# Level products of the gated attention over two chunks at once, selected straight into the block diagonal matrix

## What is computed

```python
def gla_mixer(q, k, v, low, r, w_gate_up, b_gate, norm):
    # per head: S_t = exp(g_t) * S_(t-1) + k_t v_t^T ;  o_t = q_t S_t
    # g_t is a log decay for every one of the 64 key channels
    # inside a chunk: A[t, s] = sum_c q[t,c] k[s,c] exp(b[t,c] - b[s,c]) for s <= t,
    #   with b the running sum of the log decays in the chunk
    ...
y_a = gla_mixer(g_q, g_k, g_v, g_low, g_r, ...) @ w_branch_gla
y_b = swa_mixer(s_q, s_k, s_v, swa_sinks) @ w_branch_swa
y_c = pool_mixer(p_u, pool_w, pool_scale) @ w_branch_pool
gate = sigmoid(gates)
merged = gate[0] * y_a + gate[1] * y_b + gate[2] * y_c
x = x + rmsnorm(merged @ w_out)
```

## Time and profile before

| | |
|---|---|
| median of 3 runs | 1386.88 us |
| span of the profiled execution | 1384.7 us |
| profiled execution with what lies around its span | not listed apart; the median of the runs is 2.2 us above the span |
| TensorE busy | 1376.5 us (99%) |
| VectorE busy | 846.0 us (61%) |
| ScalarE busy | 603.8 us (44%) |
| GpSimd busy | 180.3 us (13%) |
| levels of the first pair of heads | 184 to 211 us from the span's start |
| levels of the second pair | 256 to 281 us |

### The profile page before, as it was taken

The page is one execution under the profiler, slowest core; times in us unless marked ns, Lnnn a source line. Parts: engine busy times, 40 slices in busy tenths (PEclk is TensorE's granted clock), DMA queues, the critical chain, the costliest instruction groups (busy, mean ns, idle before and its releaser), DMA issues.

```text
span 1384.7 us, 17291 instructions
## 1 busy us (share of the span) xinstructions
PE 1376.5 (99%) x6788; PEld 1121.1 (81%) x6788; DVE 846.0 (61%) x1231; ACT 603.8 (44%) x923; POOL 180.3 (13%) x149
## 2 busy tenths in 40 slices
PE   9999999999999999999999999999999999999998
PEld 8777777778888888888888887888888888788887
DVE  6565565855343798623776456646455575877775
ACT  5354432433235564423444345434544445344551
POOL 0300010212212300000000122000001220243330
PEclk9999999999999999999999999999999999999999
DMA  6322222223252423333233324322124233222132
GB/s 211 120 77 76 77 62 77 77 77 90 93 171 88 137 92 113 98 109 90 93 93 106 107 77 153 109 90 76 62 62 167 87 109 113 92 61 60 48 137 76
DMA packets 37553, 135.38 MB, mean 98 GB/s; under 512 B 4432, under 2 KB 5344, under 8 KB 36960
## 3 DMA queue, kind: packets, MB, share of 16 engines
q1 hardware_dynamic: 37328, 134.28, 30.7%
q10 hardware_dynamic: 144, 0.00, 0.0%
HBM read 127.97 MB, written 6.29 MB: 97 GB/s over the span
## 4 chain that ended last, share of the span: by engine, by line
PE 91%; DVE 6%; issue 1%; ACT 1%; DMA 0%; POOL 0%; DVEq 0%; ACTq 0%; SPq 0%; POOLq 0%
PE ps L204 89%; PE ps L208 3%; DVE TT L163 2%; DVE WL L151 2%; DVE HL L163 1%; DVE X L151 1%; DVE KT L163 0%; DVE sm L169 0%; DMA raw<-in_wall 0%; ACT HH L201 0%; ACT VT L201 0%; ACT WH L188 0%; DVE QT L163 0%; DVE KT L151 0%; ACT sm L201 0%
## 5 line engine op out<-in xcount | busy, mean ns | idle before, releaser
L204 PE MATMUL ps<-HH,WH 128*128 128x512 f32 (+1 forms) x1096 | 438.0, 401 | 0.7 <-DVE HL L163 0.6
L204 PE MATMUL ps<-HH,WL 128*128 128x512 f32 (+1 forms) x1096 | 424.1, 389 | 0.0
L204 PE MATMUL ps<-HL,WH 128*128 128x512 f32 (+1 forms) x1096 | 423.3, 388 | 0.0
L151 DVE TENSOR_TENSOR WL<-raw,WH 128x1024 fp32r<-128x1024 f32 (+1 forms) x223 | 286.2, 1288 | 79.7 <-ACT WH L188 78.5
L188 ACT CAST WH<-raw 128x1024 fp32r<-128x1024 f32 (+1 forms) x222 | 230.9, 1042 | 131.3 <-PE ps L204 109.2
L204 PEld LDWEIGHTS ps<-HH,WH 128*128 128x128 f32 x1096 | 205.9, 188 | 49.6 <-issue 7.9
L204 PEld LDWEIGHTS ps<-HH,WL 128*128 128x128 f32 x1096 | 205.8, 188 | 43.6
L204 PEld LDWEIGHTS ps<-HL,WH 128*128 128x128 f32 x1096 | 206.2, 188 | 41.3 <-issue 1.7
L204 PE MATMUL ps<-PH,WH 128*128 128x512 f32 x424 | 167.5, 395 | 0.0
L204 PE MATMUL ps<-PH,WL 128*128 128x512 f32 x424 | 165.2, 390 | 0.0
L204 PE MATMUL ps<-PL,WH 128*128 128x512 f32 x424 | 165.1, 389 | 0.0
(11 more groups left out here) (221 smaller groups left out, 1454.7 us busy)
## 6 DMA issues: line engine op xcount, KB each, us to landing
raw<-in_wall SPq DMA_DIRECT2D x221, 512.0 KB, 3.6
kept<-PW SPq DMA_DIRECT2D x2, 2048.0 KB, 8.9
PWR<-kept SPq DMA_DIRECT2D x2, 2048.0 KB, 7.6
X<-in_xT SPq DMA_DIRECT2D x8, 256.0 KB, 4.2
X<-in_xT SPq DMA_DIRECT2D x4, 512.0 KB, 5.0
out_T<-X SPq DMA_DIRECT2D x7, 256.0 KB, 2.0
pe<-in_pT SPq DMA_DIRECT2D x2, 512.0 KB, 5.1
DM<-in_dm SPq DMA_DIRECT2D x1, 640.0 KB, 3.9
```

What stands on the lines that cost most here:

```text
L151: return self.put(None if self.e is None else self.e.tensor_tensor(out, x, y, op))
L204: return self.put(None if self.e is None else self.e.matmul(out, l, r, start=start, stop=stop, skip_group_check=True))
```

## The change

What it does:

- PE takes one product for two neighbouring chunks of a head: 64 key channels, 128 keys, 128 queries. There are 4 products a head and level where there were 8, each with four times the results; half of these, keys of one chunk with queries of the other, are thrown away by the mask. The two heads of the pair take turns, product by product, in place of one after the other. A head's result fills its bank, 128 partitions by 512 columns.
- DVE picks with masks of 128 x 128 straight into gAbd, 512 columns an instruction. Level 0 multiplies by the identity of 128 columns that the kernel has anyway and so writes the zeros too. gA, idm, ACT's four copies and POOL's clearing of gAbd are gone. DVE's first picking of the second pair waits until PE has read gAbd of the first (`go`, 1), where it waited for ACT's copy.
- The masks are 384 KB in place of 192 KB. SP issues their load 16 units of raw weights later, on a semaphore of their own; it is no longer among the opening loads.
- The buffers move within the same area: FA stays where it was, others shift by 1280 bytes.

The diff, cut to its core:

```diff
-        lvm = at("lvm", [P, 6, 64], I32)
-        idm = at("idm", [P, 64], F32)
+        lvm = at("lvm", [P, 6, P], I32)
...
-        A_t = at("gA", [P, 2, 4, 64], F32, o2 + 8192)
-        Abd = at("gAbd", [P, 2, 4, P], F32, o2 + 10240)
+        Abd = at("gAbd", [P, 2, 4, P], F32, o2 + 8192)
...
-                        for e_ in range(2):
-                            s = p.fill(SB[e_ + 2 * ((lv + pr) % 2)], ("gl", pr, lv, e_))
-                            if lv == 0:
-                                p.wait_ge(S.dve, "gk", pr)
-                            else:
-                                p.wait_ge(S.dve, "qks", pr, lv - 1)
-                            pp = slice(64 * e_, 64 * e_ + 64)
-                            for ch in range(8):
-                                tc = slice(64 * ch, 64 * ch + 64)
-                                p.matmul(s[64 * (ch % 2):64 * (ch % 2) + 64, 64 * (ch // 2):64 * (ch // 2) + 64],
-                                         ka[pp, tc], qa[pp, tc], True, True)
-                            p.then_inc(("gl", pr, lv, e_))
+                        two = [p.fill(SB[e_ + 2 * ((lv + pr) % 2)], ("gl", pr, lv, e_)) for e_ in range(2)]
+                        if lv == 0:
+                            p.wait_ge(S.dve, "gk", pr)
+                        else:
+                            p.wait_ge(S.dve, "qks", pr, lv - 1)
+                        for t in range(4):
+                            tc = slice(t * P, (t + 1) * P)
+                            for e_ in range(2):
+                                pp = slice(64 * e_, 64 * e_ + 64)
+                                p.matmul(two[e_][:, tc], ka[pp, tc], qa[pp, tc], True, True)
+                                if t == 3:
+                                    p.then_inc(("gl", pr, lv, e_))
...
-                        p.wait_ge(S.act, "abd", pr)
+                        p.wait_ge(S.dve, "ga", pr, 6, e_)
...
                             if lv == 0:
                                 if pr:
-                                    v.wait_ge(S.act, "abd", 0)
-                                v.wait_ge(S.consts, "consts")
-                                m = idm.rearrange("p (o i) -> p o i", o=1).to_broadcast([P, 4, 64])
-                                v.tensor_tensor(A_t[:, e_, :, :], x, m, MUL)
+                                    v.wait_ge(S.pe, "go", 1)
+                                v.wait_ge(S.ident, "ident")
+                                m = ident.rearrange("p (o i) -> p o i", o=1).to_broadcast([P, 4, P])
+                                v.tensor_tensor(Abd[:, e_, :, :], x, m, MUL)
                             else:
-                                m = lvm[:, lv - 1:lv, :].to_broadcast([P, 4, 64])
+                                m = lvm[:, lv - 1:lv, :].to_broadcast([P, 4, P])
+                                v.wait_ge(S.masks, "masks")
                                 v.wait_ge(S.dve, "ga", pr, lv - 1, e_)
-                                v.copy_predicated(A_t[:, e_, :, :], m, x)
+                                v.copy_predicated(Abd[:, e_, :, :], m, x)
...
-                    a.wait_ge(S.dve, "ga", pr, 6, 1)
-                    a.wait_ge(S.pool, "gabd")
-                    if pr:
-                        a.wait_ge(S.pe, "go", 1)
-                    a.copy(Abd[0:64, :, :, 0:64], A_t[0:64, :, :, :]).then_inc(("abd0", pr))
-                    a.copy(Abd[64:128, :, :, 64:128], A_t[64:128, :, :, :]).then_inc(("abd", pr))
...
-                            g.memset(Abd, 0.0).then_inc("gabd")
...
-            for dst, src in ((lvm, "lvm"), (idm, "idm"), (swm, "swm"), (gup, "gup"), (plw, "plw")):
+            for dst, src in ((swm, "swm"), (gup, "gup"), (plw, "plw")):
                 s.dma_start(dst, a_in[src]).then_inc("consts", sig=S.consts, by=16)
             s.first(8, 4)
             for _ in range(11):
                 s.tile(8)
+            s.dma_start(lvm, a_in["lvm"]).then_inc("masks", sig=S.masks, by=16)
```

More of the change, by code:

```diff
@@ L55 @@
     NAMES = ("pe", "dve", "act", "pool", "whi", "wlo", "half", "raw0", "raw1", "raw2", "gain", "cvec", "ident", "consts",
-             "x0", "x1", "x2", "x3", "x4", "x5", "x6", "x7", "y0", "y1", "y2", "y3", "cmask", "rope", "e0", "e1", "kept0", "kept1",
+             "masks", "x0", "x1", "x2", "x3", "x4", "x5", "x6", "x7", "y0", "y1", "y2", "y3", "cmask", "rope", "e0", "e1", "kept0", "kept1",
              "again0", "again1", "out")
@@ L61, in __init__ @@
         (self.pe, self.dve, self.act, self.pool, self.whi, self.wlo, self.half, raw0, raw1, raw2, self.gain, self.cvec, self.ident,
-         self.consts, x0, x1, x2, x3, x4, x5, x6, x7, y0, y1, y2, y3, self.cmask, self.rope, e0, e1, kept0, kept1,
+         self.consts, self.masks, x0, x1, x2, x3, x4, x5, x6, x7, y0, y1, y2, y3, self.cmask, self.rope, e0, e1, kept0, kept1,
          again0, again1, self.out) = self.all
@@ L638, in build @@
         qks = at("gqks", [P, 2, T], F32, o2 + 4096)
-        A_t = at("gA", [P, 2, 4, 64], F32, o2 + 8192)
-        Abd = at("gAbd", [P, 2, 4, P], F32, o2 + 10240)
+        Abd = at("gAbd", [P, 2, 4, P], F32, o2 + 8192)
         khT = at("gkhT", [P, 4, P], F32, ploff + 4096)
         glow = at("glow", [16, T], F32, ploff + 6144)
-        b_t = [at("gb0", [P, T], F32, o2 + 14336), at("gb1", [P, T], F32, ploff + 6144)]
+        b_t = [at("gb0", [P, T], F32, o2 + 12288), at("gb1", [P, T], F32, ploff + 6144)]
         S_t = at("gS", [P, 8, 256], F32, phoff)
@@ L647, in build @@
         GH, GL = PH[:, 8:12, :], PL[:, 0:4, :]
-        FA = at("FA", [P, 8, T], F32, arA)
+        FA = at("FA", [P, 8, T], F32, ar + 6912)
         FB = at("FB", [P, 8, T], F32, ar)
@@ L1531, in gla_side @@
                     for lv in range(7):
-                        ps2 = psum[:, 3 + 2 * ((lv + pr) % 2):5 + 2 * ((lv + pr) % 2), 0:256].rearrange("p a (b i) -> p a b i", i=64)
+                        ps2 = psum[:, 3 + 2 * ((lv + pr) % 2):5 + 2 * ((lv + pr) % 2), :].rearrange("p a (b i) -> p a b i", i=P)
                         if lv < 5:
@@ L3203, in _layout @@
     cv[:, COL["one"]] = 1.0
-    j = np.arange(64)[:, None]
-    q = np.arange(64)[None, :]
+    j = np.arange(P)[:, None]
+    q = np.arange(P)[None, :]
     lv = []
@@ L3209, in _layout @@
         lv.append(((j // (2 * s_) == q // (2 * s_)) & (j % (2 * s_) < s_) & (q % (2 * s_) >= s_)).astype(np.int32))
-    lvm = np.tile(np.stack(lv, 1), (2, 1, 1))
-    idm = np.tile(np.eye(64, dtype=f), (2, 1))
+    lvm = np.stack(lv, 1)
     r = np.arange(P)[:, None]
@@ L3225, in _layout @@
     return {
-        "wall": wall, "cvec": cv, "ident": np.eye(P, dtype=f), "lvm": np.ascontiguousarray(lvm), "idm": idm, "swm": swm,
+        "wall": wall, "cvec": cv, "ident": np.eye(P, dtype=f), "lvm": np.ascontiguousarray(lvm), "swm": swm,
         "gup": np.ascontiguousarray(i["gla_w_gate_up"][0]),
```

## The result

The changed kernel took 1389.84 us (median of 12 runs, 1389.04 to 1390.65) beside 1386.95 us for the kernel before (12 runs): a ratio of 1.0020, 95% interval 1.0012 to 1.0027. It is slower by 2.9 us where 3.2 were forecast (1390.1 us), inside the range. Timed again beside other kernels it was 1389.62 us beside 1387.12, a ratio of 1.0018 (1.0010 to 1.0027), 2.5 us. That it is slower is clear of the noise; whether by more than 0.2% is not.

A forecast was written before the change was run, and what follows sets the result against it. PE was taken as the bound, busy 1376.5 of 1384.7 us. Products (2.7 us) and a DVE stall (0.5) bring the span to 1387.9, and 2.2 more for the median gives 1390.1 us; 8 in 10 range 1388.2 to 1391.9.

The forecast's parts named there:

- The products: PE, 14 levels over two pairs of heads: 1.09 us a level for 0.90, 2.7 us in all, bounds 2.4 to 3.2.
- the scores' records: Windowed attention's scores on PE: 8 records of the new level's shape took 0.65 us, the base for 1.09 a level.
- Interleaving the heads adds nothing: PE's levels: taking turns between heads changes no time, since the scores, two products per half, already overlap; size 0.
- The Trainium skill's rule of strict program order: PE: matmuls start and end in program order, so the scores would need 0.95 us where the trace has 0.65.
- DVE's picks: DVE's masked copies of 512 columns: 0.705 us each, 0.53 more a level, 7.4 in all; bounds 0.440 to 0.88.
- The walk of the lag: Second pair, DVE's delay followed to level 5: PE waits 0.61 us there, 0.50 more than before.
- The first rival, no stall: Second pair: new timing sets DVE and POOL apart, so PE doesn't wait at level 5; 1389.4 us, chance 20 in 100.
- The streaming rival: PE's levels: interleaved products stream without the 0.21 us in and out, 0.84 to 0.88 a level; 1386.4 us, 7 in 100.
- ACT's copies, POOL's clearing, the loads: Copies and clearing off the path: worth nothing, within 0.1 us; moved mask loads 0, bounds -0.2 and +0.3.
- The sum: Whole kernel: 2.7 us for products and 0.5 for the stall, 3.2 us; span from 1384.7 to 1387.9, median 1390.1.
- The 2.2 us that the prediction laid on top: Whole kernel: the median of the runs lies 2.2 us above the profiled span, so 1387.9 becomes 1390.1.
- The parts' bounds: Whole kernel: bounds of products, stall, copies and loads together give 2.2 to 4.7 us more, or 1389.1 to 1391.6.

The follow-up runs named there:

- wide kernel by head: Changed kernel without the turns, four 128x128 products of head 0 and then four of head 1: 1397.92 us, ratio 1.0075 to the kernel before.
- half-pick run: Changed kernel with masked copies of the second pair's levels 1 to 6 taking 256 of 512 columns: 1389.77 us, ratio 1.0016 to the kernel before.
- turns by two: Changed kernel with two products of one head, then two of the other: 1391.22 us, ratio 1.0031 to the kernel before.

## Why the prediction was right, and where not

- *The products*: right in kind and nearly in size. 1.09 us a level, as worked out from the scores' records; at the next passes the difference came to 0.17 where 0.19 was taken, 2.4 us for 2.7. The lower bound of 2.4 was the value.
- *"Interleaving the heads adds nothing"*: wrong. The scores overlap because their 4 records a half are few, not because order is free. Without turns the same products take 1.64 us, and the narrow ones 0.62 with turns for 0.90 without. The number came out since the changed kernel has the turns and the scores' shape stood for them; to that extent it was luck. It hid what the change is made of: turns, worth 14 x 0.28 = 3.9 us by their rows, and wide products that cost 14 x 0.47 = 6.6.
- *The Trainium skill's rule of strict program order* ("TensorE: Matmul & The Clock Gate", Part 3, The mechanism): rejected from the scores' rows, rightly. In the wide kernel by head, head 1's first record starts while three of head 0's wait.
- *DVE's picks*: 744 ns for 705, within the bounds. The walk of the lag gave the right wait, 0.57 us for the 0.61 worked out, and the half-pick run takes it away. Inside the walk errors cancelled: a level's two picks took 0.59 us more, not 0.53, and the scaling ahead of the first 2.15 for 2.00, but WL behind it took 1.21 where it had taken 1.54.
- *The first rival, no stall*: it happens, in one of two profiles of the changed kernel, though not because POOL's and DVE's work were set apart; they met as before, and POOL was the one held up. My argument against it, that POOL's work shifts along with DVE's, held for the time of meeting and said nothing on who is held up. By the rows the change costs 2.4 us without the stall and 2.9 with it. The measured 2.5 and 2.9 us lie there, but their intervals are far too wide to tell the two cases, and how many of the timed runs had the stall is not known.
- *The streaming rival*: wrong for wide products, which keep their 0.21 in and out (0.65 for four pairs, 1.09 for eight). What it hoped from turns is true of the narrow ones, at 0.62 for 0.90, but not by doing away with the way in and out: 8 slots of 0.058 are 0.46, and 0.16 is left over. They gain since four quarters are busy at once.
- *ACT's copies, POOL's clearing, the loads*: nothing gained, as forecast. PE's first pass starts no earlier without the 224 KB.
- *The sum*: the span came to 1388.1 us for the 1387.9 forecast, with 0.4 of it the later first pass. The 2.2 us that the prediction laid on top held 0.4 by which the profiled execution had been quicker than the median; in the lists of both kernels a run's time lies 1.8 us above its own span. These errors, with the products' 0.3, partly cancel. The parts' bounds, added plainly, give 2.0 to 5.1 us and not 2.2 to 4.7; nothing hangs on it.

What stays open: why a level's price at the next passes is 0.01 under that of its own rows, how often DVE is the one held up, and whether the opening loads have a part in when PE's first pass starts.

## What to carry to other kernels

Small products on separate parts of the array should be issued in turns, one for each part: here it was worth 0.28 us of 0.90 in a group of 16, and 0.55 in the wide form. Widening a product to halve the instructions paid nothing here: each record moved twice the columns, half of the results were thrown away, and with turns in both a level took 0.47 us more. Before one moves work off an engine with time to spare (ACT's copies) onto one that is 89% busy in that stretch, one should walk the chain between the two engines that hand a buffer back and forth: the average of 61% over the whole span says nothing of it. And a stall of half a microsecond that one profile shows may be missing in the next profile of the same kernel, so it takes more than one to price it.

## What the runs showed of the hardware

- PE does not keep program order across parts of its array, but looks ahead only so far. By the records left when the other head began (3 of 4 in the scores, 3 of 8 in the wide products by head, 6 of 16 on two quarters in the kernel before), it is one record at work and three waiting for each part. That depth is inferred from these three groups, and it alone did not forecast the level of turns by two (1.20 us, not 1.09).
- A masked copy out of PSUM costs 440 ns for 256 and 744 for 512 columns, a slope of 1.19 ns a column, against 1.04 for an addition (420 and 685).
- The same program runs in two versions of its own timing, by whether DVE or POOL is held up where both work: 1.5 us of DVE's time for 1.5 of POOL's (2.21 and 3.68).
